# The state-space stage of a hybrid decoder layer, in pairs of channel groups

## What is computed

```python
z = rmsnorm(x) @ w_in                    # q | k | v | gate A (512) | u (512) | gate B (512)
attn = sliding_window_attention(q, k, v) * silu(gate_a)
# 32 groups g of 16 channels, each with a complex diagonal state of 64
lam = exp(dt * A); Bbar = (lam - 1) / A * B
x_g[l] = lam * x_g[l-1] + Bbar @ u_g[l]
y_g[l] = Re(C @ x_g[l]) + D * u_g[l]
s = gelu(y); s = s * sigmoid(s @ w_glu + b_glu) * silu(gate_b)
out = x + concat(rmsnorm(attn), rmsnorm(s)) @ w_out
```

## Time and profile before

| | us |
|---|---|
| median of 3 runs | 1832.15 |
| lowest and highest run | 1827.09, 1833.57 |
| span of the profiled execution | 1830.4 |
| attention (0 to 739) | 739 |
| early projections (739 to 1112) | 373 |
| state-space stage (1112 to 1336.8) | 224.8 |
| late projections (1336.8 to the end) | 493.6 |

### The profile page before, as it was taken

The page is one execution under the profiler, slowest core; times in us unless marked ns, Lnnn a source line. Parts: engine busy times, 40 slices in busy tenths (PEclk is TensorE's granted clock), DMA queues, the critical chain, the costliest instruction groups (busy, mean ns, idle before and its releaser), DMA issues. The chain is left out here.

```text
span 1830.4 us, 26044 instructions
## 1 busy us (share of the span) xinstructions
PE 1761.9 (96%) x8828; PEld 1424.9 (78%) x8828; DVE 1238.1 (68%) x2892; ACT 646.1 (35%) x1682; POOL 426.7 (23%) x551
## 2 busy tenths in 40 slices
PE   6899999999999997999999998999979999999999
PEld 5677777777777775788888887777767888888886
DVE  7787888777878877565765635898756655466532
ACT  5444455445544544222212102454443212122200
POOL 2122222222222222000000033799801111111110
PEclk9999999999999999899999999999999999999999
DMA  6311221123312100433243035666574455444322
GB/s 222 120 61 61 68 84 61 61 64 119 103 61 78 52 25 27 113 97 136 83 121 131 32 115 128 164 170 168 144 157 136 107 134 134 132 139 115 107 90 66
DMA packets 198404, 191.62 MB, mean 105 GB/s; under 512 B 121344, under 2 KB 157184, under 8 KB 198272
## 3 DMA queue, kind: packets, MB, share of 16 engines
q1 hardware_dynamic: 187968, 181.53, 33.3%
q10 hardware_dynamic: 10304, 8.43, 2.2%
HBM read 130.81 MB, written 59.10 MB: 104 GB/s over the span
## 5 line engine op out<-in xcount | busy, mean ns | idle before, releaser
L1045 PE MATMUL ps_b<-b_WH,b_XH 128*128 128x512 f32 (+1 forms) x776 | 286.6, 369 | 0.7 <-issue 0.4
L1047 PE MATMUL ps_b<-b_WH,b_XL 128*128 128x512 f32 (+1 forms) x776 | 277.5, 358 | 0.0
L1046 PE MATMUL ps_b<-b_WL,b_XH 128*128 128x512 f32 (+1 forms) x776 | 276.9, 357 | 0.0
L1045 PEld LDWEIGHTS ps_b<-b_WH,b_XH 128*128 128x128 f32 x776 | 148.5, 191 | 28.6 <-issue 8.7
L1000 POOL TENSOR_TENSOR b_XL<-b_XT,b_XH 128x1024 fp32r<-128x1024 f32 x33 | 80.3, 2434 | 377.7 <-ACT b_XH L1244 324.9
L1047 PEld LDWEIGHTS ps_b<-b_WH,b_XL 128*128 128x128 f32 x776 | 148.3, 191 | 21.6
L1046 PEld LDWEIGHTS ps_b<-b_WL,b_XH 128*128 128x128 f32 x776 | 148.9, 192 | 18.6
L1310 ACT ACTIVATE b_SM<-ps_b,b_small 128x128 f32<-128x128 f32 x256 | 113.7, 454 | 111.7 <-DVE b_small L1493 109.1
L685 PE MATMUL ps_g<-w_X0H,w_nextH 128*128 128x464 f32 x320 | 122.5, 383 | 2.6 <-DVEq L734 2.6
L687 PE MATMUL ps_g<-w_X0H,w_nextL 128*128 128x464 f32 x320 | 120.4, 376 | 0.0
L686 PE MATMUL ps_g<-w_X0L,w_nextH 128*128 128x464 f32 x320 | 120.0, 375 | 0.0
(11 more groups left out here) (324 smaller groups left out, 4108.8 us busy)
## 6 DMA issues: line engine op xcount, KB each, us to landing
b_XT<-in_xb SPq DMA_DIRECT2D x33, 512.0 KB, 3.9
b_XR<-in_x SPq DMA_DIRECT2D x33, 512.0 KB, 4.9
w_XT<-in_xt SPq DMA_DIRECT2D x36, 464.0 KB, 4.4
l_X<-in_xr SPq DMA_DIRECT2D x32, 512.0 KB, 4.4
out_out<-l_OUT SPq DMA_DIRECT2D x32, 512.0 KB, 3.0
scr_gs<-e_TG SPq DMA_DIRECT2D x36, 232.0 KB, 2.0
scr_u<-w_ST SPq DMA_DIRECT2D x12, 696.0 KB, 3.5
g_U<-scr_u SPq DMA_DIRECT2D x192, 43.5 KB
```

The lines of the kernel that those rows point to most:

```text
L1045: pe.matmul(bank[:, 0:c1 - c0], XH[b][:, k, :], WH[:, k, c0:c1], start=(k == 0), stop=False)
L1046: pe.matmul(bank[:, 0:c1 - c0], XH[b][:, k, :], WL[:, k, c0:c1], start=False, stop=False)
L1047: mm = pe.matmul(bank[:, 0:c1 - c0], XL[b][:, k, :], WH[:, k, c0:c1], start=False, stop=(k == KD - 1))
```

## The change

The state-space stage goes over 16 pairs of groups. Group 2p has partitions 0 to 63 and group 2p+1 partitions 64 to 127; real and imaginary parts are two tiles (index i) along the free dimension. Sums and exchanges of parts that TensorE made with SWAP are made by GpSimd from SBUF. Matmuls that belong to one group of a pair use half the columns of the array (`chunk_inputs`) or half its rows (`outputs`, state part). The tables are made by GpSimd in the early projections, from the phasors in SBUF, stored to DRAM by SP (16 stores of 257 KB, behind the gate stores of blocks 5 to 8), and loaded in the stage. Discretize handles all groups in one pass. u is laid out so that a group's chunk inputs are loaded in two transfers. The sample states are finished at the end of the stage. Weight pieces come two per pair, in pairs 2 to 11. The diff, cut:

```diff
@@ Groups
+    def load_tables(self, sp, p):
+        if p >= self.RC:
+            sp.wait_ge(self.turned_back, p - self.RC + 1)
+        sp.dma_start(self.CS[p % self.RC][:], self.scr["cs"][p]).then_inc(self.cs_ld[p % self.RC], 16)
...
+    def diagonals(self, act, p):
...
+        for g in range(2):
+            half = slice(HD * g, HD * g + HD)
+            act.activation(b[half, :, SG * g:SG * g + SG], y[half], ACT.Copy).then_inc(self.blocks, 1)
+
+    def matrices(self, pe, p):
...
+        self.cp.wait(pe, Tile(None, p))
+        pe.wait_ge(self.blocks, 2 * (p + 1))
+        pe.matmul(kernel, b[:, 0, :], c[:, 0, 0:T * SG], start=True, stop=False)
+        pe.matmul(kernel, b[:, 1, :], c[:, 1, 0:T * SG], start=False, stop=False)
+        self.mats.mark(pe.matmul(kernel[:, 0:SG], self.SWAP[0:2 * SG, 0, 0:2 * SG], par[0:2 * SG, DD:DD + SG], start=False, stop=True))
+        pe.wait_ge(self.w_parts, 4 * (p + 1))
+        for i in range(2):
+            for a in range(2):
+                for part in range(2):
...
+                    mm = pe.matmul(inputs[:, c0:c0 + P], w[:, part, i, a, :, :].rearrange("p h t -> p (h t)"), self.SWAP[:, i * part, :],
...
+    def vectors(self, dve, p):
...
+            for a in range(2):
+                dve.tensor_tensor(w[:, part, :, a], y, at(l_ + T - 1 - 8 * a, (0, 2), (0, SG), (-1, 8)), ALU.mult).then_inc(self.w_parts, 1)
+        self.cp.mark(dve.tensor_tensor(self.Q[:, 0], at(CR, (SG, 2), (0, 17), (1, SG)), at(LR, (0, 2), (1, 17), (0, SG)), ALU.mult))
+        self.cp.link(dve, Tile(None, p), dve.tensor_tensor(self.Q[:, 1], at(CN, (SG, 2), (0, 17), (1, SG)), at(LI, (0, 2), (1, 17), (0, SG)), ALU.mult))
...
+        self.cp.link(dve, Tile(None, p), dve.tensor_tensor(self.CP[p % self.RP][:], parts[:, 0], parts[:, 1], ALU.add))
@@ state_space, GpSimd
+                def scan_inputs(p):
+                    pool.wait_ge(turned, p + 1)
+                    if p:
+                        scans.wait(pool, tile(p - 1))
+                    z_sum.mark(pool.tensor_tensor(Z[:, 0, :], TI[:, 0, 0, :], TI[:, 1, 1, :], ALU.subtract))
+                    z_sum.mark(pool.tensor_tensor(Z[:, 1, :], TI[:, 0, 1, :], TI[:, 1, 0, :], ALU.add))
+
+                def states(p):
+                    s = S[p % 2]
+                    pool.wait_ge(turned_back, p + 1)
...
+                    st_out.mark(pool.tensor_tensor(s[:, 0, 0:N], TO[:, 0, 0, :], TO[:, 1, 1, :], ALU.add))
+                    st_out.mark(pool.tensor_tensor(s[:, 1, 0:N], TO[:, 0, 1, :], TO[:, 1, 0, :], ALU.subtract))
...
+                scan_inputs(0)
+                states(0)
+                scan_inputs(1)
+                for p in range(HG):
+                    if p + 1 < HG:
+                        states(p + 1)
+                    for n in weights_of(p):
+                        low_weight(n)
+                    if p + 2 < HG:
+                        scan_inputs(p + 2)
...
@@ state_space, TensorE
+                for p in range(HG):
+                    outputs(p)
+                    if p + 2 < HG:
+                        chunk_inputs(p + 2)
+                    if p + 3 < HG:
+                        matrices(p + 3)
@@ state_space, ScalarE
+                for p in range(HG):
+                    if p + 1 < HG:
+                        sample_states(p + 1)
+                        sample_copies(p + 1)
+                    if p + 2 < HG:
+                        load_toeplitz(p + 2)
+                    final_states(p)
+                    if p + 3 < HG:
+                        sample_inputs(p + 3)
+                    y_copies(p)
+                    if p + 3 < HG:
+                        kernel_copy(p + 3)
+                        store_kernel(p + 3)
+                        input_copy(p + 3)
+                    if p + 4 < HG:
+                        groups.diagonals(act, p + 4)
+                    for n in weights_of(p):
+                        high_weight(n)
@@ state_space, VectorE
+                def turn_inputs(p):
...
+                    by_table(TI[:], V[:, :, 0:N], p).then_inc(turned, 1)
+
+                def scan(p):
+                    rho = rep_last(PAR[p % RP][:, RHO:RHO + 1], N)
...
+                    for i in range(2):
+                        z_sum.wait(dve, tile(p), i + 1)
+                        scans.mark(dve.tensor_tensor_scan(ZS[:, i, :], rho, Z[:, i, :], 0.0, ALU.mult, ALU.add))
+
+                def turn_back(p):
+                    scans.wait(dve, tile(p))
...
+                    by_table(TO[:], ZS[:], p).then_inc(turned_back, 1)
+
...
+                for p in range(HG):
+                    if p + 1 < HG:
+                        scan(p + 1)
+                        turn_back(p + 1)
+                    if p + 3 < HG:
+                        groups.vectors(dve, p + 3)
+                    if p + 2 < HG:
+                        turn_inputs(p + 2)
```

More of the change, by code:

```diff
@@ new lines, in __init__, with kernel_of @@
+        self.cs_ld = [sem(f"tables_ld{i}") for i in range(self.RC)]
+        self.cleared, self.blocks, self.w_parts = sem("diagonals_cleared"), sem("diagonals_made"), sem("input_parts")
+        self.cp, self.mats = stage("cp_steps", 3), stage("pair_matrices", 2)
+        self.scans, self.turned_back, self.y_full = stage("scans", 2), sem("scans_turned_back"), stage("y_full", 4)
+    def kernel_of(self, p):
+        c = SG * SG * p if p < self.EARLY else 0
+        return self.ps[0:2 * SG, 5, c:c + SG * SG]
@@ L770, in _ @@
                     if s == ST - 1:
-                        for t in range(3):
-                            groups.vectors(dve, t)
+                        for p in range(groups.EARLY):
+                            groups.vectors(dve, p)
                     gate_in(s, 0)
@@ L1787, in low_weight @@
                     pool.wait_ge(w_hi, n + 1)
-                    pool.tensor_tensor(low, STG[n % 4][:], high.bitcast(F32), ALU.subtract).then_inc(w_lo, 1)
-                for t in range(G):
-                    if t + 4 < G:
-                        groups.phasors(pool, t + 4)
-                    if weight_of(t) is not None:
-                        low_weight(weight_of(t))
-                    if t in (28, 29):
-                        ahead.low(pool, t - 28, P)
+                    pool.tensor_tensor(low, STG[n % 4], high.bitcast(F32), ALU.subtract).then_inc(w_lo, 1)
@@ L1979, in _ @@
+                def turn_back(p):
+                    scans.wait(dve, tile(p))
+                    if p:
+                        st_out.wait(dve, tile(p - 1))
+                    by_table(TO[:], ZS[:], p).then_inc(turned_back, 1)
                 turn_inputs(0)
+                scan(0)
+                turn_back(0)
                 turn_inputs(1)
-                scan(0)
-                groups.vectors(dve, 3)
-                for t in range(G):
-                    if t + 4 < G:
-                        groups.vectors(dve, t + 4)
-                    if t + 1 < G:
-                        scan(t + 1)
-                    if t + 2 < G:
-                        turn_inputs(t + 2)
+                groups.vectors(dve, 2)
```

811 lines of the change are left out of this document (410 added, 401 removed).

## The result

| | before | after |
|---|---|---|
| median of 4 runs, us | 1830.3 | 1879.7 |
| lowest and highest run | 1827.1, 1833.6 | 1876.0, 1883.8 |
| ratio, 95% interval | | 1.027, 1.025 to 1.030 |
| span of the profiled execution | 1830.4 | 1877.2 |
| state-space stage | 224.8 | 270.2 |

A forecast was written before the change was run, and what follows sets the result against it. Matmuls on TensorE bound the kernel before; a queue loop would bind the stage after. Start 59.6 + loops 188 + end 15.3 = 262.9 against 224.8, 38 us longer: 1868 us, range 1803 to 1892.

The forecast's parts named there:

- TensorE's new work per pair: State-space stage: TensorE's matmuls for a pair of groups take 9.6 us, 3.7 us less than before.
- halves side by side: Half-array matmuls on TensorE run two at once; the rival, that they do not, gave 1882 us, chance 0.10.
- The loop: Stage, pairs 2 to 11: GpSimd, VectorE, TensorE and ScalarE queues run in turn, 18.8 us per pair, 188 for ten.
- The matrices term: Part of the loop: TensorE's matrices with the half clock and a hop, 5.7 us.
- The clock: In each loop, matrices behind TensorE's idle time runs partly at half clock and loses 2.3 us.
- The lock: GpSimd work delays VectorE operations with both inputs in SBUF: 1.1 us in vectors, 0.5 on the first scan.
- Tables in the projections at nothing: GpSimd's 65 us of table making in the early projections lengthens nothing, since matmuls cover any VectorE delay.
- the last table store may hold the barrier 0 to 3 us: End of projections: SP's last table store, behind the last gate store, counted at 0 since matrices of pairs 0 and 1 run meanwhile.
- the start: Stage from the last projection until matrices(5) are complete and the loops begin: 59.6 us.
- The loop does not bind: Rival: VectorE sets the stage's pace at 11.9 us per pair, 1801 us in all; chance 0.20.
- The loop without the clock: Rival: TensorE stays at full speed or the lock costs nothing, 14.9 to 16.5 per loop, 1830 to 1846 us; chance 0.18.
- end: Stage after matrices(15), from outputs(13) to the last halves of outputs(15) and hops: 15.3 us.

The follow-up runs named there:

- two different cuts: Changed kernel, tables stored early, with either scan_inputs ahead of low_weight on GpSimd (1802.6 us) or high_weight ahead of y_copies on ScalarE (1798.6 us).
- the filler: Changed kernel plus 22 matmuls of 128 columns, result unread, before matrices(p) for p of 5 to 14: 1863.0 us.
- the 8-column sum: Kernel with scan_inputs ahead of low_weight and tables stored early, plus GpSimd's two states sums cut to the last 8 of 257 columns: 1787.8 us.
- the run with earlier stores: Changed kernel with SyncE storing the tables in blocks 4 to 7 of the projections in place of 5 to 8: 1871.5 us.
- one swapped call: Changed kernel with scan_inputs(p+2) ahead of low_weight(n) in GpSimd's queue: 1813.4 us; with tables stored early as well, 1802.6 us.
- a third swap: Kernel with sums and high_weight both moved ahead and tables early, plus chunk_inputs(p+2) ahead of outputs(p), turn_inputs(p+2) ahead of vectors(p+3): 1856.1 us.

## Why the prediction was right, and what it missed

- **TensorE's new work per pair** (9.6): right, 9.68; halves side by side: right, so that rival is out.
- **The loop** (18.8 us, ten times, 188): right, term by term, 184.6 in all. That it is a ring is shown by two different cuts. The matrices term (5.7) was 0.7 too high in the turn shown and 0.15 too low in the one behind it, since L497 takes 2.91 us in one and 3.78 in the other; the nine average 5.44. The first of the ten loops has no wait ahead of its matrices and so no half clock, which I overlooked: 16.3, 2.5 of the 3.4 us that the ten are below the forecast.
- **The clock** (2.3): right, 2.4 by the filler. The figure was chosen between bounds of 1.7 and 3.3 from two far rows, so its closeness is partly luck.
- **The lock** (1.1 in vectors, about 0.5 per GpSimd operation): right, 0.95, 0.48 per operation. Of the 0.5 on the scans 0.38 came: the first scan takes 1.04 beside the second sum, the second 0.66. The Trainium skill's rule that I weighed ("SBUF — State Buffer", section "SBUF: two separate sides"), the side that starts first holds the ports for the whole instruction, would give 0.64 to 0.72 for these sums; the measured delay is 0.48, and 1.08 where the low_weight takes 1.27. The delay is some 0.2 us shorter than the instruction in both. That the other side fully blocks agrees with the 8-column sum, 0.20 us alone and 0.68 beside L511, where it ends when L511 does (1235.76 and 1235.70).
- **Tables in the projections at nothing; the last table store may hold the barrier 0 to 3 us, counted at 0**: this is the step that failed. As for the projections' matmuls, it was right (373 us). But I counted only the last store. Each table's buffer waits for the store two tables earlier, and the stores stand on SyncE's queue behind the last block's u loads: 7.9 us at the barrier, 8.2 us of the time by the run with earlier stores. With it the start is 59.6 + 7.9 = 67.5, where matrices(5) were complete some 67 us after 1108.
- **The projections after the stage are not touched**: wrong by 5.4 us in the profiled execution. Their first matmuls are followed by a wait at the barrier, in the kernel before and in the changed one:

```profile
1344.36 0.47 PE L1639 MATMUL ps_g<-W_OUTH,l_AH 128*128 128x512 f32 x1 [1.66 <-PEq L135]
```

```profile
1386.89 0.48 PE L1683 MATMUL ps_g<-W_OUTH,l_AH 128*128 128x512 f32 x1 [2.83 <-PEq L138]
```

  That is 1.2 us more. The other 4.2 are in the windows of the changed kernel's first 60 us:

```profile
1378.20:1408.20 30.00, 24.48 (x98) 19.02 (x96) 15.16 (x20) 11.04 (x19) 1.96 (x3) 0.94 0.74 152
1408.20:1438.20 30.00, 22.73 (x86) 18.13 (x87) 24.33 (x34) 12.76 (x19) 7.88 (x6) 0.80 0.44 91
```

  The same windows of the kernel before have clocks of 0.98 and 0.90. With levels of 1.00 and 0.50 that is 15.6 against 7.2 us at half clock in these 60 us, and half of the difference, 4.2 us, is lost work. Some 3.4 of the 8.4 us more lie right behind the wait at the barrier, the rest behind an 8.1 us wait for l_GL that both kernels have. Why the clock fell further stays open, but it goes with the length of the wait at the barrier. In the four profiled executions of the changed kernel and its variants where TensorE waits 2.8 to 3.5 us there, the clock of the second 10 us of the stretch is 0.74 to 0.84 and the stretch takes 499.0 to 500.7; in the eight with 1.8 to 2.3 us it is 0.90 to 1.00 and the stretch takes 496.1 to 498.1. All twelve are above the 493.6 of the kernel before, of which there is one profile.
- **Rivals.** "The loop does not bind" (1801) did not happen here, and is what one swapped call makes of the change (1813.4, and 1802.6 with the tables early). "The loop without the clock" would have been 1830 to 1846; the filler, at 16.3 us per loop, ends at 1863, where the barrier (7.9), the late stretch (2.6 there) and the filler's own 5 us come on top.
- **The signs.** TensorE's waits and those of the scans came as said; the clock, 0.74 to 0.83 in stretches of 20 us, and the stage's length nearly so. "Faster iterations of about 10 us in pairs 12 to 15" did not: the last matrices(15) still come 19.1 us behind matrices(14), and what is left, 16.4 us to the stage's end, has no matrices.

Forecast and result of the stage: start 59.6 + loops 188 + end 15.3 = 262.9; measured, from the end of one matrices to that of another, 67.3 + 186.5 + 16.4 = 270.2. The start is 7.7 more, which the barrier's 7.9 covers; the loops' 1.5 less and the end's 1.1 more nearly cancel. The sum of the prediction is 1868.5 (it prints 1868.7), and the median it forecasts is 1868, though its own line on the medians gives 1870.

## What to carry to other kernels

When operations move from one in-order queue to another, write down for each queue what stands directly ahead of what, and follow the arrows around: a ring with one turn per iteration costs the sum of its parts, however idle the engines are. Here either of two swaps of independent calls, in different queues, ended it, and a third swap seems to have closed a new one. A buffer that was "made ahead and stored some time" still has to be stored: look for what stands ahead of the store on its queue in the last block before a barrier. Where TensorE waits in each iteration, see whether the matmuls behind the wait take half-clock durations, and add that to the ring.

## What I had not expected of the hardware

- A GpSimd operation of 8 columns takes 0.20 us by itself and 0.68 beside VectorE's operations with both inputs in SBUF; a delay that is moved away from vectors shows up on turn_back (1.23 to 2.11) and on the scans (1.62 to 2.66). turn_inputs, which reads PSUM, stayed at 1.22 to 1.23 us in every run. GpSimd worked beside it only one to three times per run, for up to 1.1 us, so this adds little to the earlier trace rows, where L1964 keeps its time with GpSimd beside it in 28 of 32 cases.
- Filler matmuls whose result nobody reads made an iteration 2.4 us shorter, for 5 us of TensorE's time that was idle anyway.
- The 12 stores of u with 696 KB took a median of 12.6 us from issue to landing, where they had 3.5 before; their size is the same. The cause is not shown.
